# Output layer of a pooling block: where the next input rows are loaded, and where two weight sums stand among the row work

## The chip, the cores and the metric

One core of one Trainium2 chip runs the whole program. The metric is the device time of one execution in microseconds (us). The engines are TensorE (PE in the rows, its weight loads PEld), VectorE (DVE), ScalarE (ACT), GpSimd (POOL) and SyncE (SP), which here issues almost all DMA transfers; its queue is SPq in the rows.

## What is computed

One inference step of a two-layer decoder trunk over a prompt of 2048 rows and 32 sample rows: a pooling layer, a projection to shared keys and values, a differential attention layer. The change lies where the pooling layer's output product and residual add are formed, and where the weights of the next stage are prepared beside it.

```
def pool_layer(x, buf, pos0, g_norm, w_in, w_map, scale, w_out):
    ...
    y = (mix * jax.nn.silu(z)) @ w_out
    return x + y, u_ext[:, -POOL_BUF:]

def shared_kv(x, g_norm, w_kv):
    kv = rmsnorm(x, g_norm) @ w_kv
    ...
def diff_layer(x, k, v, attend, layer_idx, g_norm, w_in, ...):
    qz = rmsnorm(x, g_norm) @ w_in
    ...
```

## The kernel before

The program is written engine by engine; every engine runs its own instructions strictly in the order written, and counters (semaphores) tie them together. The stage in question is `OutLayer`: out = x + gated @ w_out_a. The prompt is cut into 16 blocks of 128 rows, block b using buffer b mod 2 of everything. A matrix operand is used as a high and a low part, so each product is three matmuls (lines 268 to 270); a block's product is 16 x 2 x 3 = 96 matmuls of 128x512.

For each block the engines do this:

- **The gated rows** (1 MB, `load_g`, line 944) are loaded from `gatedT` to one of two buffers. ScalarE copies them to the high part (`split`, L1107), once the product two blocks earlier has let go of that buffer. VectorE subtracts to get the low part (`split`, L1159), and counts `g_lo`. The product waits for this count.
- **The product** runs on TensorE and needs split(b) and add(b-2).
- **The add** (`add`, L1165): VectorE adds the product to the input rows x in place; SP then stores the result (`step`, L1054) and, once the store has landed, loads the input rows of block b+2 into the same buffer (`load_x`, L1012).

Beside that, the weights of the next stage are prepared in 32 **items**. An item is four 128x256 pieces of `w_kv` or `w_in_b`, two DMAs of 256 KB (`load_item`, L1035); ScalarE multiplies them by the norm's gain (two instructions, L1125); VectorE forms four differences (L1183), called an item's sums here; SP stores seven pieces, 896 KB (`store_item`, L1041), to `w_fold`. Two buffers serve all items, so item x+2 is loaded only when the store of item x has landed. Blocks 1 to 12 get 3, 3, 2, 3, 3, 2, 3, 3, 2, 3, 3, 2 items (`items_of`).

The order by hand: in its turn for block b, VectorE does add(b), split(b+2), then the sums of the items of b. ScalarE does split(b+2), then the scaling of the items of b. SP stores x1 of block b, waits for split(b+2), loads the gated rows of b+4, waits for the store of x1, loads the input rows of b+2, and then goes through the items of b: store item x, wait until it has landed, load item x+2, and so on. In the text, T(b) is the time at which SP issues the last item load of its turn for block b-1, that is, the last thing before its turn for block b.

Of the kernel before, what the change touches and what calls it, by code (L numbers as in the profile page):

```python
# [926 lines left out]
class OutLayer:  # L927
# [28 lines left out]
    def run(self, nxt, before, K):  # L956
# [45 lines left out]
        def items_of(b):  # L1002

            return range(share[b], share[b + 1]) if b < 15 else range(0)
# [5 lines left out]
        def on_sp(sp):  # L1010
            def load_x(b, s):
                sp.dma_start(xs[s][:, :], D["x_prompt"][0, ds(b * P, P), :]).then_inc(x_sem[s], 16)  # L1012

            gv = D["gatedT"].rearrange("(k p) t -> p k t", p=P)
            sp.dma_start(gs[:, :, :], gv[:, :, full * P:full * P + rest]).then_inc(gs_in, 16)
            load_x(0, 0)
            load_x(1, 1)
            for j in range(CG):
                sp.dma_start(xr[j * rest:(j + 1) * rest, :], rows_x[:, j * QN:(j + 1) * QN]).then_inc(xr_in, 16)
            for i in range(2, KC // LK):  # L1020
                sp.wait_ge(w_lo, (i - 1) * LK)
                sp.wait_ge(sample_mm, i - 1)
                self.load_w(sp, i)
                if i in (3, 4):
                    sp.wait_ge(g_lo, i - 2)
                    load_g(sp, i - 1, i - 3, P)

            def load_item(x):
                kd, k, c = items[x]
                _, w, half, _ = nxt.kinds[kd]  # L1030
                if x >= 2:
                    sp.wait_ge(fold_out[x % 2], 16 * (x // 2))
                for r, at in ((k, slice(0, 8, 7)), (k + HK, slice(3, 7, 3))):
                    rows = w[r * P:(r + 1) * P, half * nxt.W:(half + 1) * nxt.W].rearrange("p (h n) -> p h n", h=2)
                    sp.dma_start(fold[x % 2][:, at, :], rows[:, :, c * FN:(c + 1) * FN]).then_inc(fold_in[x % 2], 16)  # L1035

            def store_item(x):
                kd, k, c = items[x]
                sp.wait_ge(folded, 4 * x + 4)
                at = k * HN + c * FN  # L1040
                sp.dma_start(D["w_fold"][kd].rearrange("i p n -> p i n")[:, :, at:at + FN], fold[x % 2][:, 0:7, :]  # L1041
                             ).then_inc(fold_out[x % 2], 16)

            def fold_items(b):
                for x in items_of(b):
                    store_item(x)
                    if x + 2 < len(items):
                        load_item(x + 2)

            def step(i, s, ahead, x_ahead):  # L1050

                sp.wait_ge(added, 2 * i + s + 1)
                dst = D["x1"][ds((2 * i + s) * P, P), :]
                sp.dma_start(dst, xs[s][:, :]).then_inc(out_sem[s], 16)  # L1054
                if ahead:
                    sp.wait_ge(g_lo, 2 * i + s + 3)
                    load_g(sp, 2 * i + s + 4, s, P)
                if x_ahead:
                    sp.wait_ge(out_sem[s], 16 * i + 16)
                    load_x(2 * i + s + 2, s)  # L1060

            step(0, 0, True, True)
            sp.wait_ge(w_lo, KC)
            sp.wait_ge(sample_mm, KC // LK)
            load_item(0)
            load_item(1)
            step(0, 1, True, True)
            sp.wait_ge(sample_added, 1)
            for j in range(CG):
                sp.dma_start(D["x1"][full * P:full * P + rest, j * QN:(j + 1) * QN], xr[j * rest:(j + 1) * rest, :]  # L1070
                             ).then_inc(sample_out, 16)
            fold_items(1)
            for b in range(2, full - 2):
                step(b // 2, b % 2, b + 4 < full, True)
                fold_items(b)
                if b == full - 4:
                    sp.dma_start(first_rows[0], D["x1"][0:P, :]).then_inc(row_sems[0], 16)
            sp.wait_ge(g_lo, full - 1)
            for r in (1, 2):
                sp.dma_start(first_rows[r], D["x1"][r * P:(r + 1) * P, :]).then_inc(row_sems[r], 16)  # L1080
            for s in range(2):
                sp.wait_ge(fold_out[s], 16 * (len(items) // 2))
            nxt.load_raw(sp, 0)
            nxt.load_raw(sp, 1)
            step(pairs - 1, 0, False, False)
            sp.wait_ge(out_sem[0], 16 * pairs)
            sp.dma_start(first_rows[3][:, :], D["x1"][3 * P:4 * P, :]).then_inc(row_sems[3], 16)
            sp.wait_ge(first_w_lo, 1)
            nxt.load_raw(sp, 2)
            step(pairs - 1, 1, False, False)  # L1090

        self.mm, self.added, self.full = mm, added, full
        self.first_w_lo, self.first_x_lo = first_w_lo, first_x_lo
# [8 lines left out]
        def on_act(act):  # L1102
            def split(i, s, first=0):
                act.wait_ge(g_sem[s], 16 * i + 16)
                if not (isinstance(i, int) and i == 0):
                    act.wait_ge(mm, 2 * i + s - 1)
                act.activation(gh[s][:, first:, :], gst[s][:, first:, :], ACT.Copy).then_inc(g_hi, 1)  # L1107

            act.wait_ge(g_sem[0], 16)
            act.activation(gh[0][:, 0:LK, :], gst[0][:, 0:LK, :], ACT.Copy).then_inc(g_begun, 1)  # L1110
            for k in range(KC):
                i, r = divmod(k, LK)
                if k == LK:
                    split(0, 0, LK)
                    split(0, 1)
                act.wait_ge(w_sem[i % 2], 16 * (i // 2) + 16)
                act.activation(wh[:, k, :], wst[i % 2][:, r, :], ACT.Copy).then_inc(w_hi, 1)
            def fold_items(b):
                for x in items_of(b):
                    kd, k, _ = items[x]  # L1120
                    gain = gains[nxt.kinds[kd][3]]
                    act.wait_ge(fold_in[x % 2], 32 * (x // 2) + 32)
                    for r, at in ((k, slice(0, 8, 7)), (k + HK, slice(3, 7, 3))):
                        w = fold[x % 2][:, at, :]
                        act.activation(w, w, ACT.Copy, scale=gain[:, r:r + 1]).then_inc(fold_scaled, 1)  # L1125

            for b in range(2, full):
                split(b // 2, b % 2)
                fold_items(b - 2)
            def row_square(r):  # L1130
                act.wait_ge(row_sems[r], 16)
                if r:
                    act.wait_ge(row_squared, r)
                act.activation(junk, first_rows[r][:, :], ACT.Square, accum_out=row_stats[:, r:r + 1]).then_inc(row_squared, 1)

            def row_sqrt(r):
                act.wait_ge(row_mean, r + 1)
                act.activation(row_stats[:, 8 + r:9 + r], row_stats[:, 4 + r:5 + r], ACT.Sqrt).then_inc(row_root, 1)

            act.wait_ge(g_lo, full)  # L1140
            row_square(0)
            row_sqrt(0)
            for r in (1, 2):
                row_square(r)
            for r in (1, 2):
                row_sqrt(r)
            act.wait_ge(nxt.raw_in[0], 16)
            act.wait_ge(mm, full - 1)
            act.activation(first_wh[:, :, :], nxt.raw[0][:, :, :], ACT.Copy).then_inc(first_w_hi, 1)
            row_square(3)  # L1150
            row_sqrt(3)
            for r in range(2):
                act.wait_ge(first_turned, r + 1)
                act.activation(nxt.first_x[0][:, :, r * P:(r + 1) * P], first_banks[r][:, :, :], ACT.Copy).then_inc(first_x_hi, 1)

        def on_dve(dve):
# [5 lines left out]
            def add(i, s):  # L1162
                dve.wait_ge(mm, 2 * i + s + 1)
                dve.wait_ge(x_sem[s], 16 * i + 16)
                dve.tensor_tensor(xs[s][:, :], acc[s][:, :], xs[s][:, :], ALU.add).then_inc(added, 1)  # L1165
# [3 lines left out]
            for k in range(KC):  # L1169
# [3 lines left out]
                    split(0, 1)  # L1173
                dve.wait_ge(w_hi, k + 1)
                dve.tensor_tensor(wl[:, k, :], wst[i % 2][:, r, :], f32(wh[:, k, :]), ALU.subtract).then_inc(w_lo, 1)
            def fold_items(b):
                for x in items_of(b):
                    f = fold[x % 2]
                    dve.wait_ge(fold_scaled, 2 * x + 2)
                    for step, (out, a, c) in enumerate(((2, 7, 0), (4, 6, 7), (1, 6, 2), (5, 3, 1))):  # L1180
# [8 lines left out]
            dve.wait_ge(sample_mm, KC // LK)  # L1189
            dve.wait_ge(xr_in, 16 * CG)  # L1190
            dve.tensor_tensor(xr[:, :], sample_acc[:, :], xr[:, :], ALU.add).then_inc(sample_added, 1)
            fold_items(1)
            for b in range(2, full - 2):
                add(b // 2, b % 2)
                split(b // 2 + 1, b % 2)
                fold_items(b)
            def row_average(r):
                dve.wait_ge(row_squared, r + 1)
                dve.tensor_scalar(row_stats[:, 4 + r:5 + r], row_stats[:, r:r + 1], 1.0 / N, EPS, ALU.mult, ALU.add
# [1922 lines left out]
```

## Time and profile before

| | |
|---|---|
| time, median of 3 runs | 2968.87 us (2966.39 to 2971.01) |
| the profiled execution's own time | 2971.35 us |
| its span | 2969.7 us |
| TensorE busy | 2880.2 us, 97% of the span |
| VectorE, ScalarE, GpSimd busy | 61%, 47%, 4% |
| granted TensorE clock, mean | 0.991 of full |

The span is what the profile covers, 1.65 us less than the execution's own time. A busy share says how long an engine had an instruction under way, not that it limits the time. A row of the chain of waits or the timeline tells what ended an engine's idle time, with the idle time in brackets. Matmuls overlap, so their starts, not their durations, tell the pace.

### The profile page before, as it was taken

Reading aid. Unit: us, or ns where it says so; the run is one execution under the profiler, and the core shown is the slowest. Engines: PE = TensorE matmul, PEld = TensorE weight load, DVE = VectorE, ACT = ScalarE, POOL = GpSimd, SP = SyncE. Lnnn points to the kernel's source line nnn. Section 1 sums busy time; section 2 is a strip of 40 time slices with the busy share of each in tenths; the row PEclk is TensorE's granted clock in tenths of the full one; section 3 lists DMA queues with packets and bytes.
Section 4 is the critical chain, followed back from the end, with each engine's and each line's share of the span. In section 5 each row is a group of like instructions: output and inputs, shape, how many; then the busy total and the mean of one; then the engine's idle time right before and its main releaser. Section 6 shows DMA issues by size and latency. Waiting matters only on the chain. (4 is left out here: it accounts for less than half of the span.)

```text
span 2969.7 us, 45966 instructions
## 1 busy us (share of the span) xinstructions
PE 2880.2 (97%) x17242; PEld 2418.4 (81%) x17242; DVE 1802.3 (61%) x2770; ACT 1401.6 (47%) x2232; POOL 128.4 (4%) x171
## 2 busy tenths in 40 slices
PE   8999999999989999999999999999999999988998
PEld 7888888888977887778888888889999999865787
DVE  3356556464443232376767666588888888644654
ACT  4444344342222222355646454377777777533322
POOL 0000000000000000000000000100000000022211
PEclk9999999999999999999999999999999999999999
DMA  7433433432526777698897878863544444399453
GB/s 254 161 116 121 155 120 116 156 123 100 197 74 216 243 247 244 230 302 288 274 300 253 274 259 252 259 159 86 114 101 111 101 110 117 131 416 405 160 187 107
DMA packets 326493, 567.27 MB, mean 191 GB/s; under 512 B 26761, under 2 KB 205561, under 8 KB 305689
## 3 DMA queue, kind: packets, MB, share of 16 engines
q1 hardware_dynamic: 324257, 564.61, 58.8%
q8 instruction: 120, 1.97, 0.3%
q14 instruction: 68, 0.56, 0.1%
q0 software_dynamic: 2048, 0.14, 0.0%
HBM read 424.69 MB, written 140.70 MB: 190 GB/s over the span
## 5 line engine op out<-in xcount | busy, mean ns | idle before, releaser
L2197 ACT ACTIVATE attn_scores<-attn_scores,attn_lowest 128x1024 f32<-128x1024 f32 (+15 forms) x256 | 306.7, 1202 | 2.7 <-DVE attn_lowest L2255 2.7
L2255 DVE CUSTOM_DVE_ANT_0 attn_scores<-attn_s,region_early 128x1024 f32<-128x1024 f32 (+7 forms) x256 | 216.7, 856 | 69.1 <-PE attn_s L2138 38.8
L268 PE MATMUL outa_acc<-outa_w_hi,outa_g_hi 128*128 128x512 f32 x512 | 203.9, 398 | 21.0 <-DVE outa_g_lo L1159 11.3
L268 PE MATMUL pool_acc<-pool_odd_x_hi,pool_wh 128*128 128x512 f32 (+1 forms) x640 | 223.2, 349 | 0.0
L270 PE MATMUL pool_acc<-pool_odd_x_hi,pool_wl 128*128 128x512 f32 (+1 forms) x640 | 222.9, 348 | 0.0
L269 PE MATMUL pool_acc<-pool_odd_x_lo,pool_wh 128*128 128x512 f32 (+1 forms) x640 | 222.9, 348 | 0.0
L269 PE MATMUL outa_acc<-outa_w_lo,outa_g_hi 128*128 128x512 f32 x512 | 202.2, 395 | 0.0
L270 PE MATMUL outa_acc<-outa_w_hi,outa_g_lo 128*128 128x512 f32 x512 | 201.7, 394 | 0.0
L268 PE MATMUL pool_acc<-even_x,pool_wh 128*128 128x512 f32 x512 | 200.1, 391 | 0.0
L270 PE MATMUL pool_acc<-even_x,pool_wl 128*128 128x512 f32 x512 | 199.3, 389 | 0.0
L269 PE MATMUL pool_acc<-even_x,pool_wh 128*128 128x512 f32 x512 | 199.2, 389 | 0.0
L1568 ACT ACTIVATE proj_w_hi<-region_early 128x2048 fp32r<-128x2048 f32 x74 | 141.8, 1916 | 96.0 <-PE proj_acc_b L1848 35.2
L2274 DVE SCALAR_TENSOR_TENSOR attn_scores<-attn_scores,attn_coef 128x1024 f32<-128x1024 f32 (+15 forms) x128 | 173.1, 1352 | 4.5
L1671 DVE TENSOR_TENSOR proj_w_lo<-region_early,proj_w_hi 128x2048 fp32r<-128x2048 f32 x74 | 168.5, 2284 | 5.0 <-ACT proj_w_hi L1568 4.7
L2151 PE MATMUL attn_t<-all_ident,attn_scores 128*128 128x128 f32 x1088 | 162.4, 274 | 6.0 <-ACT attn_aT L2210 2.7
L1183 DVE TENSOR_TENSOR region_early<-region_early 128x256 f32<-128x256 f32 x128 | 48.7, 422 | 196.1 <-ACT region_early L1125 194.9
L621 ACT ACTIVATE pool_gates<-pool_acc 128x512 f32<-128x512 f32 (+1 forms) x64 | 38.7, 605 | 244.9 <-PE pool_acc L270 244.9
L2167 PE MATMUL attn_o<-region_early,attn_aT 128*128 128x128 f32 x1120 | 150.6, 275 | 0.0
L2151 PEld LDWEIGHTS attn_t<-all_ident,attn_scores 128*128 128x128 f32 x1088 | 127.8, 141 | 24.4 <-issue 14.0
L2167 PEld LDWEIGHTS attn_o<-region_early,attn_aT 128*128 128x128 f32 x1120 | 143.3, 191 | 4.0
L2167 PE MATMUL attn_o<-region_early,region_slot 128*128 128x128 f32 x1056 | 144.2, 275 | 1.0 <-ACT region_slot L2210 1.0
L2167 PEld LDWEIGHTS attn_o<-region_early,region_slot 128*128 128x128 f32 x1056 | 136.5, 191 | 6.7 <-ACT region_slot L2210 1.2
(364 smaller groups left out, 6962.7 us busy)
## 6 DMA issues: line engine op xcount, KB each, us to landing
region_early<-w_fold SPq DMA_DIRECT2D x110, 1024.0 KB, 6.9
pool_wz<-in_w_in_a SPq DMA_DIRECT2D x18, 2048.0 KB, 8.0
pool_wu<-w_mix SPq DMA_DIRECT2D x16, 2048.0 KB, 7.9
hold_kq<-in_cache_k SPq DMA_DIRECT2D x64, 512.0 KB, 6.9
region_early<-in_cache_v SPq DMA_DIRECT2D x60, 512.0 KB, 6.7
w_fold<-region_early SPq DMA_DIRECT2D x32, 896.0 KB, 5.6
region_early<-gatedT SPq DMA_DIRECT2D x16, 1024.0 KB, 7.8
gatedT<-pool_gates SPq DMA_DIRECT2D x48, 256.0 KB, 2.2
```

The source lines that it names most:

```text
L268: pe.matmul(out, ah, bh, start=first, stop=False)
L269: pe.matmul(out, ah, bl, start=False, stop=False)
L270: return pe.matmul(out, al, bh, start=False, stop=last)
L621: act.activation(sz[j % 2][:, 0:N].rearrange("p (c n) -> p c n", c=NCH), a[:, 0:NCH, 0:CW], ACT.Silu).then_inc(taken_act, 1)
L1183: dve.tensor_tensor(f[:, out, :], f[:, a, :], f[:, c, :], ALU.subtract).then_inc(folded, 1)
L1568: act.activation(wh[n % NW][:, :, :], self.raw[s][:, :, :], ACT.Copy).then_inc(w_hi, 1)
L1671: dve.tensor_tensor(wl[n % NW][:, :, :], self.raw[self.raw_slot(n)][:, :, :], f32(wh[n % NW][:, :, :]), ALU.subtract).then_inc(w_lo, 1)
L2151: last = pe.transpose(t_ps[idx % 2][:, kb % QUAD, :], sc[u % NSC][:, 0, a0 + kb * P:a0 + (kb + 1) * P], K["ident"][:, :])
L2167: last = pe.matmul(o_ps[r], at[idx % NAT][:, kb % QUAD, :], v[h % 2][:, kb, :], start=kb == 0, stop=kb == n - 1)
L2197: act.activation(part, part, ACT.Exp, scale=-1.0, bias=low[s][:, x:x + 1], accum_out=sums[s][:, i:i + 1]).then_inc(expd, 1)
L2255: dve.tensor_tensor_reduce(sc[s][:, c, a0:a0 + n], s_ps[idx % 2][:, at0:at0 + n], bias[h % 2][:, b0:b0 + n], -SCALE, low[s][:, x - 2:x - 1 ...
L2274: dve.scalar_tensor_tensor(out=sc[s][:, 0, part], in0=sc[s][:, 1, part], scalar=coef[s][:, r:r + 1], in1=sc[s][:, 0, part], op0=ALU.mult, ...
```

## The change

Three orders are changed; no operation is added or dropped.

- On SP the load of the input rows of block b+2, with its wait for the store of x1, moves from before the items of block b to behind them (`next_x`). At the start of the stage it moves behind the first two item loads.
- On VectorE the sums of the first two items of block b move ahead of add(b) and split(b+2).
- On ScalarE the scaling of the same two items moves ahead of split(b+2).

```
-            def step(i, s, ahead, x_ahead):
+            def step(i, s, ahead):
...
-                if x_ahead:
-                    sp.wait_ge(out_sem[s], 16 * i + 16)
-                    load_x(2 * i + s + 2, s)
+            def next_x(b):
+                sp.wait_ge(out_sem[b % 2], 16 * (b // 2) + 16)
+                load_x(b + 2, b % 2)
...
             for b in range(2, full - 2):
-                step(b // 2, b % 2, b + 4 < full, True)
+                step(b // 2, b % 2, b + 4 < full)
                 fold_items(b)
+                next_x(b)
...
             for b in range(2, full):
+                fold_items(items_of(b - 2)[:2])
                 split(b // 2, b % 2)
-                fold_items(b - 2)
+                fold_items(items_of(b - 2)[2:])
...
             for b in range(2, full - 2):
+                fold_items(items_of(b)[:2])
                 add(b // 2, b % 2)
                 split(b // 2 + 1, b % 2)
-                fold_items(b)
+                fold_items(items_of(b)[2:])
```

The first piece of the diff and the two lines with `next_x` are SP's, the second loop is ScalarE's, the third VectorE's.

VectorE, blocks 2 to 4, before. outa_x is the add, outa_g_lo the split, and four rows of region_early are one item's sums.

```order
L1183 TENSOR_TENSOR region_early<-region_early 128x256 x12
L1165 TENSOR_TENSOR outa_x0<-outa_acc0,outa_x0 128x1024
L1159 TENSOR_TENSOR outa_g_lo0<-region_early,outa_g_hi0 128x2048
L1183 TENSOR_TENSOR region_early<-region_early 128x256 x12
L1165 TENSOR_TENSOR outa_x1<-outa_acc1,outa_x1 128x1024
L1159 TENSOR_TENSOR outa_g_lo1<-region_early,outa_g_hi1 128x2048
L1183 TENSOR_TENSOR region_early<-region_early 128x256 x8
L1165 TENSOR_TENSOR outa_x0<-outa_acc0,outa_x0 128x1024
```

The same place after the change:

```order
L1188 TENSOR_TENSOR region_early<-region_early 128x256 x20
L1170 TENSOR_TENSOR outa_x0<-outa_acc0,outa_x0 128x1024
L1164 TENSOR_TENSOR outa_g_lo0<-region_early,outa_g_hi0 128x2048
L1188 TENSOR_TENSOR region_early<-region_early 128x256 x12
L1170 TENSOR_TENSOR outa_x1<-outa_acc1,outa_x1 128x1024
L1164 TENSOR_TENSOR outa_g_lo1<-region_early,outa_g_hi1 128x2048
L1188 TENSOR_TENSOR region_early<-region_early 128x256 x8
L1170 TENSOR_TENSOR outa_x0<-outa_acc0,outa_x0 128x1024
```

In front of the first add there are now the sums of five items instead of three: those of block 1 and the first two of block 2. From there on add and split always stand two items further back.

SP, the turn of block 4, before. x<-outa_x is the store of x1, gatedT the gated rows, outa_x<-in_x_prompt the input rows, w_fold<-region_early an item's store and in_w_in_b its two loads.

```order
L1054 DMA x<-outa_x 128x1024
L944 DMA region_early<-gatedT 128x16x128
L1012 DMA outa_x<-in_x_prompt 128x1024
L1041 DMA w_fold<-region_early 128x7x256
L1035 DMA region_early<-in_w_in_b 128x2x256 x2
L1041 DMA w_fold<-region_early 128x7x256
L1035 DMA region_early<-in_w_in_b 128x2x256 x2
L1041 DMA w_fold<-region_early 128x7x256
L1035 DMA region_early<-in_w_in_b 128x2x256 x2
```

The same turn after the change:

```order
L1054 DMA x<-outa_x 128x1024
L944 DMA region_early<-gatedT 128x16x128
L1041 DMA w_fold<-region_early 128x7x256
L1035 DMA region_early<-in_w_in_b 128x2x256 x2
L1041 DMA w_fold<-region_early 128x7x256
L1035 DMA region_early<-in_w_in_b 128x2x256 x2
L1041 DMA w_fold<-region_early 128x7x256
L1035 DMA region_early<-in_w_in_b 128x2x256 x2
L1012 DMA outa_x<-in_x_prompt 128x1024
```

Only the load of the input rows has moved, to the end of the turn.

## Rows read from the trace of the kernel before

**Rows 1.** Windows: the stage, and one product inside it

```profile
928.20:1250.00 321.80, 311.21 (x1351) 255.97 (x1352) 101.04 (x171) 74.32 (x93) 0.00 (x0) 0.98 0.75 245
...
1130.10:1151.90 21.80, 21.73 (x90) 17.90 (x91) 6.38 (x11) 5.58 (x7) 0.00 (x0) 0.93 0.79 251
```

Columns: stretch, its length, busy time of PE, PEld, DVE, ACT and POOL (x instructions), the granted clock, the DMA engines' share and GB/s.

**Rows 2.** Waits in 860 to 1260 us: total, times, longest

```profile
PE outa_acc L268 <- DVE outa_g_lo L1159: 11.3, 5, 4.0
...
SPq L1035 <- DMA w_fold<-region_early: 170.1, 30, 7.4
SPq L1012 <- DMA x<-outa_x: 54.0, 13, 7.2
```

**Rows 3.** Timeline of PE at product ends and late starts: start, duration, [idle]

```profile
1104.13 0.49 PE L268 MATMUL outa_acc<-outa_w_hi,outa_g_hi 128*128 128x512 f32 x1 [1.58 <-DVE outa_g_lo L1159]
...
1125.79 0.39 PE L270 MATMUL outa_acc<-outa_w_hi,outa_g_lo 128*128 128x512 f32 x1
1130.16 0.79 PE L268 MATMUL outa_acc<-outa_w_hi,outa_g_hi 128*128 128x512 f32 x1 [3.99 <-DVE outa_g_lo L1159]
...
1204.04 0.50 PE L268 MATMUL outa_acc<-outa_w_hi,outa_g_hi 128*128 128x512 f32 x1 [3.14 <-DVE outa_g_lo L1159]
```

**Rows 4.** Timeline of SP: T(8), its turn for block 8, T(9)

```profile
1106.64 0.88 SPq L1035 DMA_DIRECT2D region_early<-in_w_kv  x2
1107.56 0.47 SPq L1054 DMA_DIRECT2D x<-outa_x  x1
1108.07 0.43 SPq L944 DMA_DIRECT2D region_early<-gatedT  x1
1112.13 0.61 SPq L1012 DMA_DIRECT2D outa_x<-in_x_prompt  x1
1112.78 0.43 SPq L1041 DMA_DIRECT2D w_fold<-region_early  x1
1119.73 0.89 SPq L1035 DMA_DIRECT2D region_early<-in_w_kv  x2
...
1132.84 0.88 SPq L1035 DMA_DIRECT2D region_early<-in_w_kv  x2
```

**Rows 5.** Timeline of ACT and DVE in the same turn

```profile
1110.61 1.34 ACT L1125 ACTIVATE region_early<-region_early,all_gain_kv 128x512 f32<-128x512 f32 x2 [5.03 <-DMA region_early<-in_w_kv]
1111.98 1.56 DVE L1183 TENSOR_TENSOR region_early<-region_early 128x256 f32<-128x256 f32 x4 [4.81 <-ACT region_early L1125]
...
1125.22 1.55 DVE L1183 TENSOR_TENSOR region_early<-region_early 128x256 f32<-128x256 f32 x4 [11.69 <-ACT region_early L1125]
1126.69 1.22 DVE L1165 TENSOR_TENSOR outa_x<-outa_acc,outa_x 128x1024 f32<-128x1024 f32 x1
1127.83 2.28 DVE L1159 TENSOR_TENSOR outa_g_lo<-region_early,outa_g_hi 128x2048 fp32r<-128x2048 f32 x1
```

**Rows 6.** Timeline: start of the stage on ACT and SP, then T(2) and T(12)

```profile
926.52 1.92 ACT L1107 ACTIVATE outa_g_hi<-region_early 128x2048 fp32r<-128x2048 f32 x1 [0.80 <-PE outa_acc L270]
...
928.48 2.60 SPq L1012 DMA_DIRECT2D outa_x<-in_x_prompt  x1
...
937.10 1.34 ACT L1125 ACTIVATE region_early<-region_early,all_gain_kv 128x512 f32<-128x512 f32 x2 [8.66 <-DMA region_early<-in_w_kv]
...
942.22 0.42 SPq L1041 DMA_DIRECT2D w_fold<-region_early  x1
946.95 0.91 SPq L1035 DMA_DIRECT2D region_early<-in_w_kv  x2
...
960.53 0.88 SPq L1035 DMA_DIRECT2D region_early<-in_w_kv  x2
...
1206.38 0.88 SPq L1035 DMA_DIRECT2D region_early<-in_w_in_b  x2
```

**Rows 7.** DMA issues in 928 to 1250 us: KB each, median us to landing

```profile
w_fold<-region_early SPq DMA_DIRECT2D x32, 896.0 KB, 5.6
region_early<-gatedT SPq DMA_DIRECT2D x12, 1024.0 KB, 7.8
```

More of the change, by code:

```diff
@@ L1057, in step @@
                     load_g(sp, 2 * i + s + 4, s, P)
-                if x_ahead:
-                    sp.wait_ge(out_sem[s], 16 * i + 16)
-                    load_x(2 * i + s + 2, s)
-            step(0, 0, True, True)
+            def next_x(b):
+                sp.wait_ge(out_sem[b % 2], 16 * (b // 2) + 16)
+                load_x(b + 2, b % 2)
+            step(0, 0, True)
             sp.wait_ge(w_lo, KC)
@@ L1066, in on_sp @@
             load_item(1)
-            step(0, 1, True, True)
+            next_x(0)
+            step(0, 1, True)
             sp.wait_ge(sample_added, 1)
@@ L1072, in on_sp @@
             fold_items(1)
+            next_x(1)
             for b in range(2, full - 2):
-                step(b // 2, b % 2, b + 4 < full, True)
+                step(b // 2, b % 2, b + 4 < full)
                 fold_items(b)
+                next_x(b)
                 if b == full - 4:
@@ L1084, in on_sp @@
             nxt.load_raw(sp, 1)
-            step(pairs - 1, 0, False, False)
+            step(pairs - 1, 0, False)
             sp.wait_ge(out_sem[0], 16 * pairs)
@@ L1089, in on_sp @@
             nxt.load_raw(sp, 2)
-            step(pairs - 1, 1, False, False)
+            step(pairs - 1, 1, False)
         self.mm, self.added, self.full = mm, added, full
@@ L1117, in on_act, with fold_items @@
                 act.activation(wh[:, k, :], wst[i % 2][:, r, :], ACT.Copy).then_inc(w_hi, 1)
-            def fold_items(b):
-                for x in items_of(b):
+            def fold_items(some):
+                for x in some:
                     kd, k, _ = items[x]
@@ L1175, in on_dve, with fold_items @@
                 dve.tensor_tensor(wl[:, k, :], wst[i % 2][:, r, :], f32(wh[:, k, :]), ALU.subtract).then_inc(w_lo, 1)
-            def fold_items(b):
-                for x in items_of(b):
+            def fold_items(some):
+                for x in some:
                     f = fold[x % 2]
@@ L1191, in on_dve @@
             dve.tensor_tensor(xr[:, :], sample_acc[:, :], xr[:, :], ALU.add).then_inc(sample_added, 1)
-            fold_items(1)
+            fold_items(items_of(1))
             for b in range(2, full - 2):
+                fold_items(items_of(b)[:2])
                 add(b // 2, b % 2)
                 split(b // 2 + 1, b % 2)
-                fold_items(b)
+                fold_items(items_of(b)[2:])
             def row_average(r):
```

## The prediction

> **What bounds the kernel now.** I read the windows first, to see what TensorE could win. The change touches only the output layer's stage; there, from 928.2 to 1250.0 us, TensorE is busy 311.2 of 321.8 us [rows 1], so 10.6 us are idle. The waits say who ends them: the low half of the gated rows, VectorE's part of split(b), comes late five times, 11.3 us together [rows 2]. TensorE's timeline shows them late in the stage: products 10, 11 and 14 start after 1.58, 3.99 and 3.14 us of idleness [rows 3]; product 13 has a like one. A product without a wait lasts from 1104.13 to one step behind 1125.79, 21.9 us. Each long wait costs more than it lasts: in the 21.8 us behind the one of 3.99 us the granted clock is 0.93 [rows 1], that is 3 us at 1.2 GHz instead of 2.4, which loses 1.5 us. Four stalls are so worth about 10.6 + 4 x 1.4 = 16 us. More than that this change cannot win.
>
> Why is the split late? VectorE's timeline has, in block 8's turn, the third item's sums at 1125.22, right behind them add(9) at 1126.69 and split(11) at 1127.83, and then TensorE starts product 11 at 1130.16 [rows 3, 5]. The sums had waited 11.69 us for data that SP requested at 1119.73 [rows 4]. So SP's queue sets the pace. From T(8) to T(9), 1106.64 to 1132.84, is 26.2 us for a turn of three items [rows 4]; from T(2) to T(12), 960.53 to 1206.38, it is 245.85 us for ten turns [rows 6], 24.6 each against 21.9 for a product. The backlog grows 2.7 us a turn until TensorE feels it near block 10.
>
> SP's turn is mostly waiting: 170.1 us for item stores to land (30 times, 5.7 each) and 54.0 us for x1 stores (13 times, 4.15 each) [rows 2]. The change takes the second kind away.
>
> **The change, part by part.** *Before*, a turn goes: T(8) 1106.64, store of x1 1107.56, gated rows 1108.07, wait, input rows 1112.13, first item store 1112.78, first item load 1119.73 [rows 4]. From T to the item store it is 6.1 us. A later item costs (1132.84 - 1119.73) / 2 = 6.55 us [rows 4], of which the load takes 0.9 to issue, so a later store is waited for 5.6 us. The ten turns hold seven threes and three twos, thus 17 later items, 111.4 us. The other 134.5 us are 13.45 a turn from T to the first item load, of which the first store's wait is 13.45 - 6.1 = 7.3 us.
>
> *Removed:* 4.15 us of waiting for x1's store. Behind the items it has landed long ago; only the load's 0.4 us of issue stay.
>
> *Added:* add(b) now stands behind the sums of the first two items of b, and the second of these is the very item that SP loads at T(b): with two buffers the loads of turn b-1 are for the items two places on. Before, SP's next turn didn't wait for that data. Now it goes so: load at T, ScalarE begins to scale at T + 4.0 (1110.61), VectorE its sums at T + 5.35 (1111.98), and add and split follow as they follow sums now, 1.47 and 1.14 us on, at T + 6.8 and T + 7.95 [rows 4, 5]. The add is done at T + 8.1, and only then may SP store x1. The split takes 2.28 us [rows 5] and is done at T + 10.3; ScalarE's half, 1.92 us behind the scaling, is ready by T + 7.3. SP holds the next gated rows' load for this split, issues it at T + 10.3, and the first item store at T + 10.8 instead of T + 6.1. The wait of 4.15 us is replaced by two of 9 us together. Behind them on SP are queued the item stores and loads, and on these wait the next two items' sums, the next add, the next split: a ring through SP, the DMA, ScalarE and VectorE.
>
> *The first item store's wait* has no row in this order. Ahead of the store lies now the whole megabyte of gated rows, 0.5 us old; before it was half a megabyte of input rows, and gated rows 4.7 us old. Lowest: 5.6 us, as for a later store. Highest: the gated rows land first, 7.8 - 0.5, and the store takes its own 5.6 behind them [rows 7], 12.9 us. I take 8.0, near the 7.3 of the row most like it, plus some for the larger part of the megabyte still to come. T to the first item load becomes 10.8 + 8.0 = 18.8 us, 5.35 more a turn (ends 2.95 and 10.25).
>
> What a store has ahead of it does count in the rows: 6.95 us with rows ahead of it (1112.78 to 1119.73), 5.6 with only an item's load [rows 4]. The Trainium skill, page "DMA: Bandwidth & Descriptors", section "Queues, rings and completion order", says that SP's transfers share one ring on each DMA engine and that descriptors are consumed in ring order. By that rule putting the store right behind a megabyte speaks against the change; taken strictly it gives the high end, 49 us above my sum, and the two waits in the rows agree with its direction.
>
> *Start of the stage.* The first two items are requested at 928.5, where the input rows' load stood, and I estimate that their data come 1.5 us sooner than for the scaling at 937.10 [rows 6], at 935.6. But split(3), which ScalarE did at 926.52 [rows 6], now stands behind both scalings: 935.6 + 2 x 1.34 + 1.92 + 2.28 is about 942.4 at its end on VectorE. SP's next gated rows, the sample rows' stores and the first item store wait for it: about 944.7 instead of 942.22, and then 7.0 us, as a first store behind gated rows, instead of 4.7 (to 946.95) [rows 6]. The two items after it cost 6.3 each: T(2) is 964.4, 3.9 later.
>
> *At no cost:* the third item's load, scaling and sums (4.0 + 1.35 + 1.5) are hidden by the second item's store and load but for 0.3 us. The moved input rows have a whole product, 21.9 us, in which to land. VectorE is busy 101 of 322 us [rows 1]: for it only the order counts.
>
> *The end.* Before, product 14 starts at 1204.04, T(12) - 2.3, since its split stood behind the third item of block 11 alone. Now it is T(12) + 10.3, 12.6 later.
>
> **Sum.** T(12) = 1206.4 + 3.9 + 10 x 5.35 = 1263.8; product 14 starts at 1274.1, 70.1 us later. What follows is the same, its slow start too. TensorE is no bound: a turn is now 31.6 us, or 25.0 with two items, against 21.9 + 1.5. From the profiled execution's own 2971.35 us this gives 3041.4; it lies 2.5 us above the median of the runs, so the median becomes **3039 us**, 2.4% more.
>
> **The rivals.** *The wait is gone and TensorE is the bound; faster.* A turn of 24.6 - 4.15 = 20.4 us is below a product's 21.9; nothing is late and the 16 us come back: 2953. It needs split(b+2) before the end of product b+1, so the comparison that decides is T(2) + 10.3 = 974.7 against product 3's end, 928.2 + 2 x 21.8 = 971.8 [rows 1]: late at the first turn, with no backlog yet. Item data would have to land 3 us sooner than in any such row. 4%.
>
> *Removed and added wait cancel within a turn.* If first store and new chain together took 5.35 us less than I say, the turn would stay as it is; the start and the end still move by 3.9 and 12.6: 2985. 4%. Within 6 us of now needs still more: 2%.
>
> *Light queue.* With the input rows gone from the middle the first store takes 5.6 us: 3.9 + 29.5 + 12.6 = 46, so 3015. Against it: the gated rows are right ahead. For times from 2990 to 3018, 9%.
>
> *Strict queue.* The store waits 12.9 us, +10.25 a turn, 119 us: 3088. No row shows transfers without overlap. Above 3056: 6%.
>
> The forecast's own case, 3018 to 3056, has 75%.
>
> **Range and chances.** From just below the light queue's 3015 to 3056, which is a first store's wait of 9.7 us: some 8 in 10. A measurement of this kernel can't tell under 0.2%, 6 us, from no change. Faster 4%, within it 2%, slower 94%.
>
> **What would show it.** TensorE's wait for the low half of the gated rows, 11.3 us now, becomes 60 to 75 us in eleven cases, from product 4 on (3 us there), then some 8 in turns of three items and 2 in turns of two. SP's wait for x1's store goes from 54 us to nearly none, and one for the add, some 7 us a turn, appears. SP's timeline shows x1's store at T + 8.1, gated rows at T + 10.3 and 31.6 us between the T's. If x1's store follows T within 2 us in the middle turns, the ring isn't closed and I am wrong; if the ring is there and the first item store is waited for 5.6 or 12 us, only the size is wrong.

## The result and the profile after

Timed on one chip, the kernel before takes 2970.36 us in the median of six runs (2966.39 to 2973.65) and the changed one 3033.49 us (3030.36 to 3036.26). The ratio is 1.0216 (95% interval 1.0204 to 1.0227): slower by 2.2%, some 63 us. The profiled execution of the changed kernel took 3033.92 us with a span of 3032.2 us and a mean granted clock of 0.982; the span grew by 62.5 us. One execution each of kernels 11 and 12 below took 6250 and 3611 us, far outside all others: their ratios leave it out, and without it their medians would be 2961.7 and 2951.9 us instead of 2963.12 and 2952.62. The names are those of before, the lines some four further on: sums L1188, add L1170, split L1111 and L1164, scaling L1129.

Windows of the changed kernel: the same stage, from its start to the same distance (62.7 us) behind the old end, and one product. The columns are those of [rows 1].

```profile
928.20:1312.70 384.50, 324.12 (x1347) 263.24 (x1348) 101.08 (x171) 75.89 (x93) 0.00 (x0) 0.92 0.62 205
1150.31:1172.00 21.69, 21.69 (x90) 17.86 (x91) 3.04 (x8) 2.68 (x4) 0.00 (x0) 0.93 0.70 225
```

The stage has 60.4 us without a matmul where it had 10.6 [rows 1], and its matmuls are busy 12.9 us longer, at a granted clock of 0.92 where it was 0.98. The two together are the 62.7 us. The DMA engines did less than before on the mean (share 0.62, was 0.75): over the stage as a whole it wasn't bandwidth that ran short, things were waiting for one another.

Waits of the changed kernel, 860 to 1330 us: total, times, longest.

```profile
PE outa_acc L268 <- DVE outa_g_lo L1164: 61.3, 13, 9.0
```

The same view for SP's queue alone:

```profile
SPq L1035 <- DMA w_fold<-region_early: 155.5, 30, 5.9
SPq L1054 <- DVE outa_x L1170: 116.3, 14, 19.3
...
SPq L944 <- DVE outa_g_lo L1164: 31.6, 12, 10.6
SPq L1012 <- DMA x<-outa_x: 7.8, 2, 6.9
```

Against [rows 2], TensorE's wait for the low half went from 11.3 to 61.3 us, and SP's wait for the landing of x1 from 54.0 to 7.8 us. SP's waits for the add grew from 32.9 us (3 cases, the same view of the kernel before) to 116.3 in 14, those for the split from 2.7 us (one case) to 31.6 in 12.

Timeline of SP, changed kernel, from T(8) to T(9), to be laid beside [rows 4]:

```profile
1140.12 0.88 SPq L1035 DMA_DIRECT2D region_early<-in_w_kv  x2
1141.05 0.47 SPq L1012 DMA_DIRECT2D outa_x<-in_x_prompt  x1
1148.01 0.36 SPq L1054 DMA_DIRECT2D x<-outa_x  x1
1150.21 0.38 SPq L944 DMA_DIRECT2D region_early<-gatedT  x1
1150.63 1.84 SPq L1041 DMA_DIRECT2D w_fold<-region_early  x1
1158.00 0.89 SPq L1035 DMA_DIRECT2D region_early<-in_w_kv  x2
...
1170.75 0.88 SPq L1035 DMA_DIRECT2D region_early<-in_w_kv  x2
```

VectorE in the same turn, and then ScalarE, beside [rows 5]:

```profile
1145.29 1.55 DVE L1188 TENSOR_TENSOR region_early<-region_early 128x256 f32<-128x256 f32 x4 [4.65 <-ACT region_early L1129]
1146.77 1.22 DVE L1170 TENSOR_TENSOR outa_x<-outa_acc,outa_x 128x1024 f32<-128x1024 f32 x1
1147.90 2.28 DVE L1164 TENSOR_TENSOR outa_g_lo<-region_early,outa_g_hi 128x2048 fp32r<-128x2048 f32 x1
```

```profile
1143.93 1.33 ACT L1129 ACTIVATE region_early<-region_early,all_gain_kv 128x512 f32<-128x512 f32 x2 [4.87 <-DMA region_early<-in_w_kv]
1145.17 1.89 ACT L1111 ACTIVATE outa_g_hi<-region_early 128x2048 fp32r<-128x2048 f32 x1
```

The ring can be read off in one pass. SP loads the second item at 1140.12; ScalarE scales it 3.8 us later; VectorE forms its sums at 1145.29 and right behind them does the add and the split, which is over at 1150.2. SP has two transfers that wait for these two: x1's store goes at T + 7.9 and the gated rows at T + 10.1. Only then is the first item store issued, and the item load behind it needs that store to land, at T + 17.9, where before it was T + 13.1. TensorE pays at product ends. Its late starts:

```profile
977.29 0.79 PE L268 MATMUL outa_acc<-outa_w_hi,outa_g_hi 128*128 128x512 f32 x1 [5.35 <-DVE outa_g_lo L1164]
...
1119.91 0.50 PE L268 MATMUL outa_acc<-outa_w_hi,outa_g_hi 128*128 128x512 f32 x1 [1.03 <-DVE outa_g_lo L1164]
1150.31 0.79 PE L268 MATMUL outa_acc<-outa_w_hi,outa_g_hi 128*128 128x512 f32 x1 [8.31 <-DVE outa_g_lo L1164]
...
1266.57 0.79 PE L268 MATMUL outa_acc<-outa_w_hi,outa_g_hi 128*128 128x512 f32 x1 [5.86 <-DVE outa_g_lo L1164]
```

### The profile page after: what moved, and what is told of

It reads as the page before. It is cut to its first block and busy times, and to the rows that moved or that the text cites. A ratio compares the mean times of both kernels' runs of the same rounds, so it can differ in the third digit from the quotient of the medians.

```text
span 3032.2 us, 45966 instructions
## 1 busy us (share of the span) xinstructions
PE 2894.3 (95%) x17242; PEld 2428.8 (80%) x17242; DVE 1799.0 (59%) x2770; ACT 1401.4 (46%) x2232; POOL 134.1 (4%) x171
## 5 line engine op out<-in xcount | busy, mean ns | idle before, releaser
L268 PE MATMUL outa_acc<-outa_w_hi,outa_g_hi 128*128 128x512 f32 x512 | 210.2, 411 | 70.9 <-DVE outa_g_lo L1164 61.3
L1188 DVE TENSOR_TENSOR region_early<-region_early 128x256 f32<-128x256 f32 x128 | 48.6, 421 | 236.2 <-ACT region_early L1129 235.1
L268 PEld LDWEIGHTS outa_acc<-outa_w_hi,outa_g_hi 128*128 128x128 f32 x512 | 100.9, 197 | 101.1 <-DVE outa_g_lo L1164 41.2
```

The source lines that it names most:

```text
L268: pe.matmul(out, ah, bh, start=first, stop=False)
L1188: dve.tensor_tensor(f[:, out, :], f[:, a, :], f[:, c, :], ALU.subtract).then_inc(folded, 1)
```

## The experiments

The table has every run. The texts set off below are what was expected of each before it ran. "Turn" is (T(12) - T(2)) / 10, and "first load" the mean distance from T(b) to the first item load of the turn, both read off SP's timeline. What a turn has behind that first load is 10.8 to 11.6 us in all kernels but 4 and 12, so what separates these kernels happens between T and the first load. Kernel 4 has two items of each turn in another place, so its 10.74 is not to be compared. The ratio is to the kernel before on the same chip.

| kernel | median us | ratio (95%) | turn | first load |
|---|---|---|---|---|
| before | 2970.4 | 1 | 24.59 | 13.58 |
| the change | 3033.49 | 1.0216 (1.0204 to 1.0227) | 28.93 | 18.03 |
| 1 rows only | 2971.56 | 1.0001 (0.9992 to 1.0010) | 24.65 | 13.81 |
| 2 order only | 3053.75 | 1.0277 (1.0261 to 1.0293) | 30.97 | 20.14 |
| 3 one item ahead | 2977.47 | 1.0022 (1.0013 to 1.0031) | 24.36 | 13.39 |
| 4 SP follows | 3003.64 | 1.0106 (1.0090 to 1.0121) | 25.87 | 10.74 |
| 5 ScalarE only | 3033.07 | 1.0209 (1.0193 to 1.0225) | 28.79 | 17.93 |
| 6 VectorE only | 3029.93 | 1.0193 (1.0177 to 1.0208) | 29.08 | 18.13 |
| 7 store first | 3000.06 | 1.0106 (1.0091 to 1.0121) | 26.01 | 14.85 |
| 8 half the rows | 2952.80 | 0.9935 (0.9920 to 0.9950) | 23.34 | 12.32 |
| 9 rows from ScalarE | 2966.58 | 0.9985 (0.9976 to 0.9994) | 24.19 | 12.59 |
| 10 third item later | 2965.28 | 0.9980 (0.9970 to 0.9991) | 24.66 | 13.61 |
| 11 and the last items | 2963.12 | 0.9968 (0.9956 to 0.9980) | 24.66 | 13.62 |
| 12 all | 2952.62 | 0.9939 (0.9926 to 0.9952) | 21.72 | 8.05 |

The theory to test is that of the prediction: the loss comes from the second item's sums ahead of add and split, and the moved input rows by themselves are a gain. The rival explanations are that the loss lies with the moved load, or with one engine's order alone.

### 1. The input rows moved, the orders of ScalarE and VectorE left

```
                 if ahead:
                     sp.wait_ge(g_lo, 2 * i + s + 3)
                     load_g(sp, 2 * i + s + 4, s, P)
-                if x_ahead:
-                    sp.wait_ge(out_sem[s], 16 * i + 16)
-                    load_x(2 * i + s + 2, s)
...
                 fold_items(b)
+                next_x(b)
```

> Only SP's part of the change: the input rows' load moves behind the items; VectorE and ScalarE keep the old order. Ring theory (the loss comes from add and split standing behind the item that is loaded last in the turn before): no ring, first item store at T + 1.9, its wait 7.4 to 8.0 as in the changed kernel, so a turn averages 20.5 to 21.3 us, below a product's 21.9; TensorE's wait for the low half falls under 3 us and the time is about 2955 (2950 to 2963). Queue theory (the loss comes from the item store right behind a megabyte of rows and from the input rows behind the item load): most of the loss stays, over 3000.

Measured: 2971.56 us, no difference from before: neither the gain of the ring theory nor the loss of the queue theory. The wait for x1 is gone and bought nothing. Timeline of SP in kernel 1:

```profile
1106.67 0.88 SPq L1035 DMA_DIRECT2D region_early<-in_w_kv  x2
1107.60 0.47 SPq L1012 DMA_DIRECT2D outa_x<-in_x_prompt  x1
1108.11 0.43 SPq L1054 DMA_DIRECT2D x<-outa_x  x1
1108.58 0.43 SPq L944 DMA_DIRECT2D region_early<-gatedT  x1
1109.06 6.13 SPq L1041 DMA_DIRECT2D w_fold<-region_early  x1
1120.67 0.89 SPq L1035 DMA_DIRECT2D region_early<-in_w_kv  x2
```

The item store's issue starts 3.7 us earlier than in [rows 4], as meant, but it takes 6.13 us instead of 0.43, and the store lands 11.6 us behind its start instead of 7.0. The first load comes at T + 14.0; before it was T + 13.1. The windows of that stretch say why, in the kernel before and then in kernel 1:

```profile
1106.64:1119.73 13.09, 13.09 (x60) 10.83 (x59) 2.01 (x6) 1.34 (x2) 0.00 (x0) 1.00 0.84 270
```

```profile
1106.67:1120.67 14.00, 14.00 (x63) 11.61 (x62) 2.00 (x6) 1.34 (x2) 0.00 (x0) 1.00 0.80 253
```

The last number, GB/s, times the length is 3.53 and 3.54 MB. That is what SP requests in the stretch: an item's load, the input rows, x1, the gated rows and an item's store, 512 + 512 + 512 + 1024 + 896 KB. So when the store landed, all that had been requested ahead of it had moved, in both orders. That alone does not say that the bytes set the time, since the changed kernel moves the same 3.54 MB between T(8) and its first load:

```profile
1140.12:1158.00 17.88, 9.57 (x37) 7.50 (x36) 5.34 (x8) 3.13 (x3) 0.00 (x0) 0.81 0.60 198
```

What differs is the rate: the DMA engines' share is 0.60 there, and 0.84 and 0.80 before and in kernel 1. And through SP's wait for x1's store, in the kernel before, they were as busy as anywhere in the turn:

```profile
1107.56:1112.13 4.57, 4.57 (x22) 3.79 (x21) 0.15 (x1) 1.34 (x2) 0.00 (x0) 1.00 0.89 281
```

So the wait that the change removes lay over work that has to be done anyway before the next load. Run 8 tests this by taking some of the work away.

### 2. The orders changed, the input rows still ahead of the items

```
             for b in range(2, full - 2):
                 step(b // 2, b % 2, b + 4 < full)
-                fold_items(b)
                 next_x(b)
+                fold_items(b)
```

> Only VectorE's and ScalarE's part: sums and scaling of two items ahead of add and split; SP keeps the input rows' load ahead of the items (at the start of the stage it stays behind the first item loads). Ring theory: x1's store at T + 8, landing about T + 12.3, input rows, first item store at T + 12.9 instead of T + 10.5, so 2.4 us more a turn than the changed kernel and about 3057 (3045 to 3065). Queue theory: about the time before, 2970.

Measured: 3053.75 us, as expected. The orders alone cost 83 us, and in their presence the moved input rows are worth 20 us, 2 us a turn: there the DMA engines have room in the first 8 us of a turn (in the changed kernel their share is 0.40 from 1140.12 to 1148.01 us), so rows requested early find room, and do not stand ahead of the store. The way there was not the expected one: SP's wait for x1's store to land, which was to cost the 2.4 us, is all but absent here too (9.1 us in two cases). In block 8's turn the input rows' issue takes 1.80 us and the item store, at T + 11.9 instead of T + 10.5, lands after 8.1 instead of 7.4.

### 3. One item ahead instead of two

```
-                fold_items(items_of(b - 2)[:2])
+                fold_items(items_of(b - 2)[:1])
                 split(b // 2, b % 2)
-                fold_items(items_of(b - 2)[2:])
+                fold_items(items_of(b - 2)[1:])
```

and the same on VectorE.

> The changed kernel with one item's sums and scaling ahead of add and split instead of two. That item is loaded one place before T, some 6.4 us earlier, and is summed at about T + 0.5. Ring theory: add(b) is ready by T + 1.7, the ring is open, a turn is near 21 us, time 2955 to 2965. Rival (sums ahead of the add cost by being ahead, about in proportion to their number): half the loss, about 3000.

Measured: 2977.47 us. The ring is gone: turn 24.36 us, and the loss falls from 63 to 7 us. It is the second item, the one loaded at T(b), that closes it. The expected gain over before fails for the reason of run 1: the same bytes go before the first item's store lands, first load 13.39. What is left of the loss stands at the two ends: T(2) is 3.3 us later than before (963.8), and the split of product 14 begins at 1209.04, 7.3 us later.

### 4. SP's order follows VectorE's

```
             for b in range(2, full - 2):
+                fold_items(items_of(b)[:2])
                 step(b // 2, b % 2, b + 4 < full)
-                fold_items(b)
+                fold_items(items_of(b)[2:])
                 next_x(b)
```

> The changed kernel with SP's order made to follow VectorE's: SP stores the first two items of the block (and loads the next two) before its step for x1 and the gated rows, the third item after it. Two items still stand ahead of the add. Ring theory: the first item store goes at T + 1.4, the add at T + 7 is met while SP waits for item stores anyway; a turn is 23 us with three items and some 19.5 with two, about a product's 21.9 on the mean; what stays is the first stall of 5 to 7 us at product 4: 2960 to 2972. Rival (order on VectorE alone costs): 3033 stays.

Measured: 3003.64 us, a miss. SP no longer waits for add and split ahead of items, and half of the loss is gone (turn 25.87), but not more. Timeline of SP from the gated rows' load in block 8's turn on:

```profile
1141.94 0.43 SPq L944 DMA_DIRECT2D region_early<-gatedT  x1
1142.42 4.16 SPq L1041 DMA_DIRECT2D w_fold<-region_early  x1
1152.90 0.89 SPq L1035 DMA_DIRECT2D region_early<-in_w_kv  x2
```

A store right behind the gated rows still lands only after 10.5 us, and the split waits for the item that is loaded behind it. VectorE in the same kernel:

```profile
1158.29 1.56 DVE L1189 TENSOR_TENSOR region_early<-region_early 128x256 f32<-128x256 f32 x4 [9.99 <-ACT region_early L1130]
1160.90 2.28 DVE L1165 TENSOR_TENSOR outa_g_lo<-region_early,outa_g_hi 128x2048 fp32r<-128x2048 f32 x1
```

The item summed at 1158.29 was requested at 1152.90; add and split follow, and the product behind them starts at 1163.23, 5.04 us late. What that late load costs was not varied by itself.

### 5 and 6. One engine's order alone

Kernel 5 keeps ScalarE's new order and gives VectorE the old one, kernel 6 the other way round:

```
             for b in range(2, full - 2):
-                fold_items(items_of(b)[:2])
                 add(b // 2, b % 2)
                 split(b // 2 + 1, b % 2)
-                fold_items(items_of(b)[2:])
+                fold_items(items_of(b))
```

```
             for b in range(2, full):
-                fold_items(items_of(b - 2)[:2])
                 split(b // 2, b % 2)
-                fold_items(items_of(b - 2)[2:])
+                fold_items(items_of(b - 2))
```

> The changed kernel with VectorE's old order: only ScalarE has the scaling of two items ahead of its split. Ring theory: the ring closes over ScalarE too, because SP holds the gated rows' load for split(b+2): scaling at T + 4.0, ScalarE's split done at T + 7.2, VectorE's at T + 9.4, gated rows at T + 9.4 instead of T + 10.2, while x1's store is free. So nearly the whole loss, 0.8 us a turn less: about 3022 (3010 to 3030). Rival (only the add's place on VectorE matters): about 2971 as in the kernel with SP's part alone.

> The changed kernel with ScalarE's old order: only VectorE has the sums ahead of add and split. Ring theory: T to x1's store 8.0 us and to the gated rows 10.2 us as in the changed kernel, since VectorE's split is the later one anyway: 3033 (3028 to 3038). Rival (both orders share the loss): near 3000.

Measured: 3033.07 and 3029.93 us. Each order alone costs nearly as much as both (63 us). The ring needs only one engine on which the split stands behind the second item. In kernel 5 I expected 11 us less. Its VectorE and SP in block 8's turn, T(8) = 1138.29:

```profile
1145.38 2.29 DVE L1164 TENSOR_TENSOR outa_g_lo<-region_early,outa_g_hi 128x2048 fp32r<-128x2048 f32 x1 [11.62 <-ACT outa_g_hi L1111]
1147.59 3.01 DVE L1188 TENSOR_TENSOR region_early<-region_early 128x256 f32<-128x256 f32 x8
```

```profile
1147.70 0.38 SPq L944 DMA_DIRECT2D region_early<-gatedT  x1
1149.16 0.75 SPq L1041 DMA_DIRECT2D w_fold<-region_early  x1
```

The gated rows do go 0.7 us earlier in the turn, at T + 9.4, but now the first item's sums stand behind the late split and hold the item store to T + 10.9.

### 7. The changed kernel, with the first item store ahead of the gated rows' load

```
                     sp.wait_ge(g_lo, 2 * i + s + 3)
+                if first is not None:
+                    store_item(first)
+                if ahead:
                     load_g(sp, 2 * i + s + 4, s, P)
```

> The changed kernel with SP's first item store ahead of the gated rows' load (both still behind the wait for the split). In the changed kernel that store waits 7.4 us behind a megabyte. If its place on the queue sets this wait, it falls to 5.6 and the gated rows fill the gaps between item store and item load: turn 1.0 to 1.8 us shorter, 3015 to 3023. Rival (the wait is the fixed cost of a store): 3033.

Measured: 3000.06 us, the direction expected and more of it: the turn is 2.9 us shorter, where 1.0 to 1.8 was expected. Only two adjacent issues on SP are exchanged:

```profile
1131.29 0.38 SPq L1041 DMA_DIRECT2D w_fold<-region_early  x1
1131.71 0.56 SPq L944 DMA_DIRECT2D region_early<-gatedT  x1
1135.85 0.89 SPq L1035 DMA_DIRECT2D region_early<-in_w_kv  x2
```

From the store's issue to the load it is now 4.6 us, where it was 7.4. The price is paid by the gated rows, median landing 7.1 us instead of 5.4, and they have most of a turn for it. By the rule of the Trainium skill, page "DMA: Bandwidth & Descriptors", section "Queues, rings and completion order", that each DMA engine takes the descriptors of one issuer in ring order, the store should gain by standing in front; the row agrees. It also shows how little of a strict queue it is: 1024 KB taken from in front of the store saved 2.8 us.

### 8. Fewer bytes ahead of the first item store

Kernel 1, with half of the gated rows' load:

```
-                    load_g(sp, 2 * i + s + 4, s, P)
+                    b, half = 2 * i + s + 4, slice(0, KC // 2)
+                    sp.dma_start(gst[s][:, half, 0:P], gv[:, half, ds(b * P, P)]).then_inc(g_sem[s], 16)
```

> The kernel with SP's part alone, but from block 4 on only half of each block's gated rows is loaded (8 of 16 slices, 0.5 MB; the other half of the buffer keeps what it held), so the output is not the reference's; its time shows what the bytes cost. Theory: with SP's part alone the removed wait only uncovered DMA time; from T to the first item load the 16 DMA engines have some 11 us of work for 2.9 MB, so 0.5 MB less takes 2 to 3 us off every turn, which falls to 21.9 or less, and the stalls go: 2955 to 2960. Rival (fixed latencies of the chained transfers set the turn): stays at 2970.

Measured: 2952.80 us, in the expected range, though not quite by the expected steps. Every instruction but that load is as in kernel 1, and the turn falls from 24.65 to 23.34 us: 1.3 us, not 2 to 3, and not to 21.9. That was enough, since a lag of 1.4 us a turn instead of 2.7 doesn't reach TensorE before the stage is over: no product from the third on starts late. So what must be moved before the first item's store lands sets the turn, and fixed latencies alone do not. Whether it is the bytes or the number of packets no run separates: from T(8) to the first load the half load takes away 0.5 of 3.5 MB, and 1024 of 3808 packets. It need not be less, only later, as run 12 shows.

### 9. The gated rows requested by ScalarE

```
                 split(b // 2, b % 2)
+                if 4 <= b < full - 2:
+                    act.wait_ge(g_lo, b + 1)
+                    load_g(act, b + 2, b % 2, P)
                 fold_items(b - 2)
```

On SP `if ahead:` becomes `if ahead and i == 0:`.

> The kernel before with the gated rows of blocks 6 to 15 loaded from ScalarE's queue, right behind its split, instead of SP's. If SP's own queue (its order and its issue) were the limit between T and the first item load, that stretch would fall by 2 to 4 us and the time to 2955 to 2960. Theory: the 16 DMA engines are shared and busy through that stretch, so the bytes cost the same from either queue: 2970 (2964 to 2974).

Measured: 2966.58 us, 0.15% less than before, first load 12.59. That is 1.0 us sooner, of which 0.6 is lost again behind it. The Trainium skill, page "DMA: Bandwidth & Descriptors", section "Issuing engines are not separate DMA queues", says that transfers from several issuers run on the same 16 DMA engines and that only issue time is saved; a turn shorter by 0.4 us, about the 0.43 us that SP took to issue this load [rows 4], agrees.

### 10 and 11. Taking the split away from the other side

Before, what makes a split late is the third item of the block before. Kernel 10 leaves SP alone and puts the third item's scaling and sums behind the next block's split:

```
                 split(b // 2 + 1, b % 2)
-                fold_items(b)
+                fold_items(items_of(b - 1)[2:])
+                fold_items(items_of(b)[:2])
```

(on VectorE; on ScalarE likewise). Kernel 11 also puts the last items behind the last splits, and the input rows of blocks 14 and 15 behind the last items on SP.

> The kernel before with a block's third item moved the other way on VectorE and ScalarE: its scaling and sums stand behind the next block's split and add instead of ahead of them. SP as before. Theory: add and split no longer stand behind data that SP has just asked for, so TensorE's four late stalls go (16 us), while SP keeps its own lag; part is given back at the end of the stage, where the next stage's first rows and weights, which SP loads behind all items, come no sooner: 2960 to 2966. Rival (SP's lag holds TensorE anyway, through the gated rows' loads): 2970.

> The kernel with the third item behind the next split, and the end of the stage reordered: the last two items' scaling and sums stand behind the last split, and SP loads the input rows of blocks 14 and 15 behind the next stage's first rows instead of ahead of them. Theory: the one stall left there (5.7 us ahead of product 15) goes and the next stage's first rows come some 7 us sooner, so product 15 and the first product of the next stage aren't held: about 2959 (2955 to 2963). Rival (the next stage's start is held by its fourth row block, which needs add(14)): 2965, no better.

Measured: 2965.28 us, in the expected range, and 2963.12 us, at the edge of it. The turn stays at 24.66 us in both: SP's pace is untouched. In kernel 10 a single late product is left (5.71 us, product 15), in kernel 11 none. Of the 16 us that the prediction put on TensorE's stalls kernel 11 recovers 7 to 8. The rest is lost right behind the stage, in the stretch from 1223 to 1260 us, in kernel 11 and then in kernel 12:

```profile
1223.00:1260.00 37.00, 32.16 (x145) 25.95 (x146) 22.06 (x25) 23.02 (x32) 0.00 (x0) 0.91 0.76 288
```

```profile
1223.00:1260.00 37.00, 35.58 (x176) 29.31 (x175) 23.21 (x22) 21.85 (x28) 0.00 (x0) 1.00 0.55 204
```

The items still end late (T(12) = 1207.0), and with them the loads that the next stage begins with.

### 12. Both: the third item later, and the store first

```
+                early = b < 12
+                step(b // 2, b % 2, b + 4 < full, b < 12, items_of(b)[0] if early else None)
+                fold_items(b, early)
```

This is kernel 11 with the exchange of kernel 7.

> The third item behind the next split and the reordered end of the stage, and on top SP's first item store of a turn ahead of the gated rows' load. In the changed kernel that one place on the queue took 3 us off the first item load of each turn. Theory: here it lets SP's lag shrink too, from 24.7 us a turn to 22 to 23, so that the items end 15 to 20 us sooner and the next stage's first rows and weights are ready when TensorE gets there; TensorE loses nothing from product 3 to the next stage: 2955 (2951 to 2959). Rival (the DMA engines are full from T to the first item load, so the order of the transfers gives nothing): 2961, as without it.

Measured: 2952.62 us, 0.61% less than before, the best of the kernels that compute the reference's output and level with kernel 8, which doesn't. Timeline of SP from T(8) to T(9), then the windows of the turn's two parts:

```profile
1091.01 0.89 SPq L1035 DMA_DIRECT2D region_early<-in_w_kv  x2
1091.94 0.47 SPq L1055 DMA_DIRECT2D x<-outa_x  x1
1092.51 0.37 SPq L1041 DMA_DIRECT2D w_fold<-region_early  x1
1092.93 1.34 SPq L944 DMA_DIRECT2D region_early<-gatedT  x1
1096.30 2.82 SPq L1012 DMA_DIRECT2D outa_x<-in_x_prompt  x1
1099.19 0.92 SPq L1035 DMA_DIRECT2D region_early<-in_w_kv  x2
...
1113.09 0.88 SPq L1035 DMA_DIRECT2D region_early<-in_w_kv  x2
```

```profile
1091.01:1099.19 8.18, 8.18 (x38) 6.78 (x37) 1.52 (x4) 1.34 (x2) 0.00 (x0) 1.00 0.87 281
1099.19:1113.09 13.90, 13.90 (x63) 11.53 (x62) 6.01 (x9) 4.48 (x5) 0.00 (x0) 1.00 0.86 297
```

The first load comes at T + 8.2 instead of T + 13.1. The same bytes move in the turn, but the gated and the input rows now go beside the later items, where the DMA engines had room: their share behind the first load is 0.86, where the kernel before had 0.66 (1119.73 to 1132.84 us). The wait for x1 is still there, 27.2 us in twelve cases, and does no harm, since the item store is under way through it: it lands 6.7 us behind its issue, at 1099.2, and SP is done with the input rows' issue at 1099.12. The turn of 21.72 us is below a product's 21.9, so TensorE is the bound: from 928.20 to 1223.00 us it is busy 294.23 of 294.80 us at a granted clock of 1.00.

## Why the prediction was right, and where it was not

The time, 3033.49 against 3039, and its cause came out as forecast. Step by step:

- **The ring** is there as written, and the timelines show every member of it: x1's store at T + 7.9 (8.1 said), gated rows at T + 10.1 (10.3), item store at T + 10.5 (10.8). Taking the second item out of it (run 3) removes 56 of the 63 us.
- **The first item store's wait** was the open cost, taken at 8.0 us between 5.6 and 12.9; it was 7.4. The 8.0 was a choice between bounds, so that it came near is in part luck. Run 7 shows what the wait is made of: without the gated rows in front it is 4.6. The high end was worked out with 7.8 us for the gated rows to land, and here they land in 5.4.
- **The turn** grew by 4.34 us, not 5.35. T to the first load was 18.03 instead of 18.8 us in the mean (the step above and 0.3 us of the chain), and the 17 later items took 6.41 instead of 6.55 each, 0.24 us a turn. Over ten turns that is 10 us less than said.
- **The start of the stage** was mis-sized the other way: T(2) came at 967.0, 6.5 us later, not 3.9. Four of its terms were off, in both directions. The split was to end at 942.4 and the gated rows' load to go then; it went at 944.84, since the first item's data came 0.9 us later than taken (ScalarE scales it at 936.46) and ScalarE had to wait another 1.5 us for the second item's (939.34). SP needs 3.03 us to issue the four stores of sample rows, where it took 1.82 before, so that the item store worked out for 944.7 goes at 948.33. That store's wait was taken at 7.0 us, as behind gated rows, and was 4.7, as before the change, which gives 2.3 us back. The two items behind cost 7.0 us each, not 6.3, most of it in the first load's issue of 1.87 us instead of 0.9.

```profile
944.84 0.38 SPq L944 DMA_DIRECT2D region_early<-gatedT  x1
945.26 3.03 SPq L1072 DMA_DIRECT2D x<-outa_x_sample  x4
948.33 0.42 SPq L1041 DMA_DIRECT2D w_fold<-region_early  x1
953.03 1.87 SPq L1035 DMA_DIRECT2D region_early<-in_w_kv  x2
```

- **The end**, 12.6 us, is 12.55: split 14 begins 7.9 us behind T(12), and began 4.7 us ahead of it.
- **The sum**: 6.5 + 43.4 + 12.6 = 62.5 us, all of the span's difference, against 70.1 said.
- **TensorE's wait**, 61.3 us, is inside the 60 to 75 said. In turns of two items the starts are late by 0.7 to 1.0 us, not 2, and product 4 by 5.35, not 3, which is mostly the start's 2.6 us again.
- **The step of the prediction that failed**, though the sum did not hang on it, is "Removed: 4.15 us of waiting for x1's store". In the kernel before this wait was worth nothing (run 1). It was a wait of SP, but the DMA engines worked through it on transfers that the next load had to await in any case. So the fast rival's turn of 20.4 us and its 2953 us had no ground, ring or no ring: with the ring open the change gives 2977 (run 3). My sum doesn't contain the 4.15 us, because I had costed the new chain from its own rows and not as before minus 4.15. Inside the ring the moved rows do save 2 us a turn (run 2).
- The bound on what TensorE could win, 16 us, held for what it covered; kernel 12 gains 18, part of it behind the stage.

What stays open is why SP needed 6.13 us to issue the store in kernel 1. The sums of that item were over at 1107.2, so it was not data. The issue takes 2.18 us with half of the gated rows in front (run 8), which would fit a queue that was full, but no run varied the number of transfers outstanding by itself. What SP's standing still costs is little: in run 8 it lasts 4.0 us less in block 8's turn, and the first load comes only 1.3 us sooner (T + 12.7 instead of T + 14.0).

## What to carry to other kernels

Before a step is put ahead of another, ask when its input was requested: an item loaded at the start of a turn must not stand ahead of work on which the same queue's next requests depend, and one engine with that order is enough to close the ring. Before a wait of the queue is removed, look at the DMA engines' share and GB/s in the stretch of that wait. In the kernel before they were at 0.89 and 281 through it, and removing it gained nothing; inside the ring, with a share of 0.40 in the first 8 us of the turn, the same move gained 2 us a turn. Where they are busy, the order of the requests is what counts: first the store that the next load waits for, then the large load that has time.

## What the runs showed of the hardware

- The issue of one 896 KB store on SP took 0.43 us in the kernel before (at 1112.78) and 6.13 us in kernel 1 (at 1109.06), there right behind 2560 KB of other requests made in 2.4 us; SP issues nothing else in that time.
- Exchanging a store of 896 KB and a load of 1024 KB issued 0.4 us apart changed the store's landing from 7.4 to 4.6 us in block 8's turn and the load's from 5.4 to 7.1 in the median (run 7).
- In a product behind 8.31 us of idleness the granted clock was 0.93 over 21.7 us, the same as behind 3.99 us [rows 1]: the longer stall did not cost more clock afterwards, and the matmuls behind it started 0.43 us apart at first and 0.23 us later.
